# Second-layer heads of a hybrid decoder step: products of the new prompt state ahead of the value products, last sample state ahead of the norm work

## The reference, cut to what matters

```python
S = jnp.einsum('bhtd,bhsd->bhts', qc, kc) * jnp.exp(Dm - m_t[..., None])
num = jnp.einsum('bhts,bhse->bhte', S, vc) + ...      # value products
qn = jnp.sum(S, axis=-1) + ...                        # row sums
h = num / jnp.maximum(jnp.abs(qn), jnp.exp(-m_t))[..., None]
C_new = ... + jnp.einsum('bhsd,bhse->bhde', kc * decay[..., None], vc)   # new prompt state
n_new = ... + jnp.einsum('bhs,bhsd->bhd', decay, kc)                     # its row
```

## Time and profile before

| what | value |
|---|---|
| median of 3 runs | 1146.53 us (1138.76 to 1151.35) |
| profiled execution | 1140.05 us, its span 1138.3 us |
| TensorE busy | 1037.9 us (91%) |
| VectorE, ScalarE, GpSimd busy | 625.8 us, 401.9 us, 309.9 us |
| granted TensorE clock, mean | 0.959 |
| second layer's heads in the span | about 548 to 1032 us |

### The profile page before, as it was taken

How to read it: one execution, slowest core, us unless ns; L and a number is a source line. 1 busy time by engine, 2 the same in 40 slices (tenths; PEclk the granted TensorE clock), 3 DMA queues, 4 the chain that set the end, 5 groups by cost and what they waited for, 6 DMA issues and landing times. The chain is left out here.

```text
span 1138.3 us, 16176 instructions
## 1 busy us (share of the span) xinstructions
PE 1037.9 (91%) x5942; PEld 742.9 (65%) x5942; DVE 625.8 (55%) x1058; ACT 401.9 (35%) x705; POOL 309.9 (27%) x208
## 2 busy tenths in 40 slices
PE   5899999998679789998797999999999999997998
PEld 3677777775325489897575385847686587635776
DVE  4546767767343579996234563454345443446332
ACT  4434434432210323334445235432544344414210
POOL 5445444341000243441522223231513132110000
PEclk9999999999889789999899899999999999897999
DMA  9243455575491144453468754867468664744221
GB/s 250 71 123 97 131 138 132 146 198 171 127 306 57 38 83 150 156 177 139 141 201 294 280 190 142 284 237 254 160 203 288 215 214 152 271 147 149 75 74 75
DMA packets 167437, 191.75 MB, mean 168 GB/s; under 512 B 23638, under 2 KB 111558, under 8 KB 165798
## 3 DMA queue, kind: packets, MB, share of 16 engines
q1 hardware_dynamic: 154654, 159.15, 44.3%
q0 software_dynamic: 6000, 24.35, 7.1%
q10 hardware_dynamic: 6712, 7.29, 1.9%
HBM read 135.66 MB, written 55.22 MB: 168 GB/s over the span
## 5 line engine op out<-in xcount | busy, mean ns | idle before, releaser
L2125 PE MATMUL col_ps<-h_hi,ring_hi 128*128 128x260 f32 x448 | 130.3, 291 | 0.0
L2125 PE MATMUL col_ps<-h_hi,ring_lo 128*128 128x260 f32 x448 | 127.9, 286 | 0.0
L2125 PE MATMUL col_ps<-low,ring_hi 128*128 128x260 f32 x448 | 127.8, 285 | 0.0
L1978 DVE SCALAR_TENSOR_TENSOR state<-state,s_all,outer 128x1024 f32<-128x1024 f32 x64 | 86.0, 1372 | 74.5 <-ACT outer L1812 54.0
L648 PE MATMUL out_ps<-w_hi_a,h_hi_a 128*128 128x512 f32 x256 | 106.4, 416 | 5.5 <-POOL w_lo_a L469 5.5
L469 POOL TENSOR_TENSOR w_lo_a<-w_in,w_hi_a 128x1024 fp32r<-128x1024 f32 x32 | 87.2, 2746 | 79.6 <-ACT w_hi_a L344 40.5
L648 PE MATMUL out_ps<-w_lo_a,h_hi_a 128*128 128x512 f32 x256 | 101.2, 395 | 0.0
L648 PE MATMUL out_ps<-w_hi_a,h_lo 128*128 128x512 f32 x256 | 101.0, 395 | 0.0
L2125 PEld LDWEIGHTS col_ps<-h_hi,ring_hi 128*128 128x128 f32 x448 | 86.1, 192 | 12.9 <-issue 12.9
L1812 ACT ACTIVATE outer<-v_bcast,k_cols 128x512 f32<-128x512 f32 x128 | 81.8, 711 | 20.9 <-DMA v_bcast<-keep_v_rows 16.2
L1431 PE MATMUL xm_ps<-h_hi_c,w_col_hi 128*128 128x260 f32 x304 | 87.7, 288 | 0.0
(11 more groups left out here) (327 smaller groups left out, 2078.0 us busy)
## 6 DMA issues: line engine op xcount, KB each, us to landing
state<-in_state_C SPq DMA_DIRECT2D x64, 512.0 KB, 6.6
out_C_sample<-state SPq DMA_DIRECT2D x64, 512.0 KB, 5.5
w_in<-in_a_w_in SPq DMA_DIRECT2D x64, 256.0 KB, 5.7
ring_raw<-in_m_w_in POOLq DMA_DIRECT2D x28, 512.0 KB, 7.7
shared<-in_m_w_in SPq DMA_DIRECT2D x20, 512.0 KB, 5.1
k_head<-in_cache_k SPq DMA_DIRECT2D x128, 64.0 KB, 1.9
v_bcast<-keep_v_rows SPq DMA_DIRECT2D x32, 256.0 KB, 8.4
keep_xm_keep<-xm SPq DMA_DIRECT2D x4, 1040.0 KB, 6.9
```

Of the source, the lines that this page charges most:

```text
L1978: nc.vector.scalar_tensor_tensor(out=state[:, i % 4], in0=state[:, i % 4], scalar=s_all[:, 0, h, b:b + 1], in1=outer[:, g], op0=ALU.mult, ...
L2125: last = nc.tensor.matmul(col_ps[:, u % 4, 0:HALF], a[n % RING][:, k, :], b[:, k, s * HALF:(s + 1) * HALF], start=(k == 0 and j == 0), sto ...
```

## The change

Three edits, in the second layer's heads alone:

- TensorE: `prompt_state` d = 0 to 3 moves ahead of `values`. Sample `b0 + 4` is then multiplied after d = 1, head 0's samples 5 and 6 after d = 3, and sample 7 after the value product t = 1. The row of the new state leaves `prompt_state` and becomes `state_row`, after the value products and ahead of `sample_sum`. It waits for the first `norm_h` only.
- The numbers: `CP` comes ahead of `NUM`, and `TOK_TURNS` likewise. Bank parities stay. GpSimd's wait for `NUM + NT` thereby covers the prompt state's products as well.
- VectorE: `new_state` of sample 7, and in head 0 of sample 6, move ahead of `norm_h` t = 0.

ScalarE's program, SyncE's program and the number of instructions stay as they are.

```diff
-    NUM = OGT + TT
-    CP = NUM + NT
-    SNUM = CP + FH
+    CP = OGT + TT
+    NUM = CP + FH
+    SNUM = NUM + NT
...
                  + ["act"] * TT
+                 + ["act"] * FH
                  + ["dve"] * NT
-                 + ["act"] * FH
...
                 if h == 0:
                     new_state(h, 5)
+                    new_state(h, 6)
+                new_state(h, 7)
                 norm_h(h, 0)
                 norm_h(h, 1)
-                if h == 0:
-                    new_state(h, 6)
                 scale_h(h, 0)
                 norm_h(h, 2)
                 scale_h(h, 1)
                 norm_h(h, 3)
                 scale_h(h, 2)
-                new_state(h, 7)
                 scale_h(h, 3)
...
                 last.then_inc(toks_done, 1)
-                if d == 0:
-                    pe.wait_ge(*tok_count(h, NUM + NT - 1))
-                    for s in range(NT):
-                        last = nc.tensor.matmul(q_ps[0:1, :], one[:], kd[:, s, :], start=(s == 0), stop=(s == NT - 1))
-                    last.then_inc(n_done, 1)
+
+            def state_row(h):
+
+                pe.wait_ge(*tok_count(h, NUM))
+                for s in range(NT):
+                    last = nc.tensor.matmul(q_ps[0:1, :], one[:], kd[:, s, :], start=(s == 0), stop=(s == NT - 1))
+                last.then_inc(n_done, 1)
...
                 for t in range(TT):
                     turned_gate(h, t)
-                for t in range(NT):
-                    values(h, t)
-                    if t == 1:
+                for d in range(FH):
+                    prompt_state(h, d)
+                    if d == 1:
                         sample_q(h, b0 + 4)
                 if h == 0:
                     sample_q(h, 5)
                     sample_q(h, 6)
-                for d in range(FH):
-                    prompt_state(h, d)
-                    if d == 1:
+                for t in range(NT):
+                    values(h, t)
+                    if t == 1:
                         sample_q(h, 7)
+                state_row(h)
                 sample_sum(h)
```

## The result

The changed kernel takes 1158.5 us (median of 4 runs, 1157.2 to 1169.4), the kernel before 1142.6 (4 runs, three of them those shown ahead of the prediction). The ratio is 1.0158, 95% interval 1.011 to 1.0205: slower by about 1.6%, some 18 us. The prediction was 1151 us with a range of 1139 to 1161; the time lies in the range, but in the part above 1%, which had a chance of 0.13.

A forecast was written before the change was run, and what follows sets the result against it. TensorE's program was taken to set the pace (452.1 of 484.0 us busy over the heads). Head 0 +3.5, heads 1 to 3 +2.7, clock −1.7 gave +4.5 us: 1151.0 us on the median, range 1139 to 1161.

The forecast's parts named there:

- The wait removed: Head 0: TensorE's idle time ahead of the third value product goes, −3.7 us, and with it some clock.
- The banks in head 0: Prompt-state products d = 2 and d = 3 wait for ScalarE to empty their banks: 6.4 and 0.8 us.
- The clock behind the wait: Head 0: lowered clock on the d = 2 prompt-state product after the bank wait, 1.5 us (bounds 0 and 3.6).
- Sample 7 ahead of the norms: Head 0: sample 7's late state updates delay the norms on VectorE and so TensorE, 1.0 us (0 to 7.6).
- the slower rival: Head 0: sample 7's state load takes over 5 us, up to 10.6, holding the norms; 1158.6 us, chance 0.12.
- The sample norm copy: All heads: `sample_sum` waits for the copy behind the last norm and scaling; 1.5 us in head 0, 0.9 in others.
- My sign of being wrong: Listed signs: no idle ahead of L2248, an output-stage wait for `w_y`, or heads 1 to 3 growing over 2 us.
- The chain of 4.4 us: Time from last value product to `sample_sum` through last norm, root, scaling and copy; `state_row` covers 3.59 of it.
- The clock given back: Heads 1 and 3: row sums now stand between dense products, so half the clock loss returns, −1.7 us (0 to −3.4).
- where I took 0.7: Head 0: charge of 0.7 us for a second fall of the clock behind the row sums.
- That transposes bring the clock down whatever follows: Rival, all heads: the clock falls on prompt-state d = 0 after the gate's turns; +7.9 us, 1154.4 us, chance 0.14.
- Transfers moved later: Later loads of `xm` and, in the last head, `w_y` are covered, the latter by some 3 us; charged 0.

The follow-up runs named there:

- the run with the copies first: Changed kernel with ScalarE's copies out of the prompt-state banks ahead of the outer products of samples 6 and 7 in head 0; 1155.7 us, 1.0101 to the kernel before.
- split first: Changed kernel with GpSimd's split of a weight tile moved ahead of the four roots; 1152.2 us, ratio 1.0051 to the kernel before.
- the early copy: Changed kernel with VectorE's copy for the sample sum moved from behind the norms to behind the second norm; 1147.2 us, ratio 1.0011 to the kernel before.
- the run with the old head 0: Changed kernel with head 0 put back in the order of before, heads 1 to 3 in the new one; 1153.6 us, ratio 1.0064 to the kernel before.

## Why the prediction was right in kind and wrong in size

**The wait removed** went as written: 3.69 us fell to 0.38.

**The banks in head 0** were the right mechanism at nearly the right price: 6.62 us measured for 6.4, 0.52 for 0.8, with the broadcasts as the cause. That ScalarE's order behind them decides was shown by the run with the copies first. The clock behind the wait was under-charged: the third product took 6.08 us, 2.5 over its 3.6, where I took 1.5.

**Sample 7 ahead of the norms** was charged 1.0 us and took about 1.9: its two products and the waits of 0.41 and 0.38 us fill 650.87 to 653.72, which is 2.85 us, and the pair takes 0.98 in heads 1 to 3, where nothing is waited for. The last loads were issued at 643.45 and 644.47 us, and VectorE had them only at 647.99 and 650.98:

```profile
647.99 1.28 DVE L1978 SCALAR_TENSOR_TENSOR state<-state,s_all,outer 128x1024 f32<-128x1024 f32 x1 [12.98 <-DMA state<-in_state_C]
650.98 1.28 DVE L1978 SCALAR_TENSOR_TENSOR state<-state,s_all,outer 128x1024 f32<-128x1024 f32 x1 [1.70 <-DMA state<-in_state_C]
```

The second took 6.5 us, past the point of 5 us that I named for the slower rival. That rival's time, 1158.6 us, is what was measured, but not for its reason: it gave this load 6.6 us of delay, and it cost 0.9 more than the 1.0 charged. The upper end of the range was drawn past that rival, so that the time lies inside it is luck.

**The sample norm copy** is the step that failed. I charged 1.5 us in head 0 and 0.9 in each of the others, 4.2 in all; measured are 3.30, 2.92, 2.92 and 1.11, 10.3 us. My sign of being wrong, a stretch in heads 1 to 3 that grows by over 2 us, came in head 2 (31.8 to 35.0). The chain of 4.4 us was put together from a head in which the last scaling came after GpSimd's split, so it held no contention; I read the root's row and not the one behind it in GpSimd's order. Head 1 before, the split and the small step of the last scaling:

```profile
762.52 2.34 POOL L1682 TENSOR_TENSOR ring_lo<-ring_raw,ring_hi 128x1024 fp32r<-128x1024 f32 x1
768.15 0.15 DVE L2011 TENSOR_TENSOR rd<-rd,rstd_ln 128x1 f32<-128x1 f32 x1
```

In the new order the split starts exactly when the last scaling wants to run. In head 3, which has no split, the charge of 0.9 was nearly right (1.11), and so was the chain: from the end of the last value product (1034.2 us) to the end of the copy (1038.6) it took 4.5 us. That the split makes the rest was shown twice: split first brings the waits to about 1 us, and the early copy takes them away with the standstill still there. The Trainium skill states the rule in "SBUF — State Buffer", section "Who interferes with whom": VectorE and GpSimd share a pair of ports, a VectorE instruction with two SBUF inputs contends with a GpSimd instruction that reads SBUF, and the order of issue decides which of the two blocks. By it the wait was to be foreseen, and the trace agrees for L2011, 2.23 us beside a split of 2.34. The trace of before held such waits too, in another place (see the last section). With the split first the waits of heads 0 to 2 are 1.23, 0.94 and 0.84 us, so the split adds 2.07, 1.98 and 2.08, some 6.1 us; and the clock behind the longer waits, 0.62 and 0.60 over 4 us in heads 0 and 2 where it is 1.00 with the split first, adds about 1.5 us in each (0.4 of 4 us).

**The clock given back** was −1.7 us. In the changed kernel the clock fell behind the row sums in heads 0 and 3 and not in 1 and 2 (the first value products take 4.52, 2.82, 2.82 and 4.52 us); before, in 0, 1 and 3 (4.12, 4.38, 2.82 and 4.52). So head 1 won what I had counted, and head 0 paid 1.7 us where I took 0.7. That transposes bring the clock down whatever follows did not show: all the first prompt-state products run at full speed in heads 0 to 2 (7.13 us a pair), and nearly so in head 3 (7.36).

**Transfers moved later** cost nothing: the first output weights were issued at 1036.90 us and took 8.3 us to land, the output stage began at 1051.42, and no wait for them appears.

In sum, head 0 was forecast at 45.6 us and took 50.5: 1.8 us more at the sample sum, 1.0 for the clock on the third product, 1.0 behind the row sums, 0.9 at sample 7, together 4.7 of the 4.9. Heads 1 to 3 were forecast at +1.0 us in all. In the traces 434.1 − 417.9 − 8.4 = 7.8 us lie outside head 0's stretch, 1.1 of them in the columns behind it and 6.7 in heads 1 to 3; the run with the old head 0 has 7.3 for these heads.

## What to carry to other kernels

When products change places on one engine, the engines that empty their banks keep their old order: write out for each bank what stands ahead of its copy, and move the copies with the products. A wait that becomes late next has to be priced in its new neighbourhood: read what every other engine does in that microsecond, GpSimd's next instruction too, not only the lengths in the old place. A result that one late consumer needs (here a 0.68 us copy) goes ahead of a chain that it does not depend on.

## What the runs showed of the hardware

A split of a 128x1024 tile on GpSimd (2.34 us) held VectorE instructions with two SBUF tensors until it was over: a product of two 128x1 columns, started 0.13 us after the split, went from 0.15 to 2.23 us. It held a product of 128x512 in the same way. The kernel before shows that in the mixing of the head, which the change did not touch. L2027 multiplies two SBUF tensors and takes 0.69 us alone; beside a split it took 2.80 in head 0. L1926 reads one tensor from SBUF and one from PSUM, where TensorE's products lie; beside a split it took 0.42 us, as it does elsewhere. VectorE, then GpSimd:

```profile
672.48 2.80 DVE L2027 SCALAR_TENSOR_TENSOR gated<-xc_head,gated 128x512 f32<-128x512 f32 x1
676.34 0.69 DVE L2027 SCALAR_TENSOR_TENSOR gated<-xc_head,gated 128x512 f32<-128x512 f32 x1
681.25 0.42 DVE L1926 SCALAR_TENSOR_TENSOR gated<-scr,col_ps 128x260 f32<-128x260 f32 x1 [2.48 <-ACT scr L1776]
```

```profile
672.33 2.40 POOL L1682 TENSOR_TENSOR ring_lo<-ring_raw,ring_hi 128x1024 fp32r<-128x1024 f32 x1 [0.60 <-ACT ring_hi L1771]
681.02 2.39 POOL L1682 TENSOR_TENSOR ring_lo<-ring_raw,ring_hi 128x1024 fp32r<-128x1024 f32 x1 [2.70 <-ACT ring_hi L1771]
```

With the product in scalar form, which read one SBUF tensor and one column scalar and took 0.21 us beside the split, the next instruction was held instead, a scaling of a 128x512 tile with one SBUF tensor and two column scalars: 2.20 us for 0.55. I had not expected that of an instruction with one SBUF tensor. The Trainium skill, "SBUF — State Buffer", section "Who interferes with whom", names `tensor_scalar`, which this scaling is, among the operations that can take the shared pair when their operands meet conditions. No run here tests whether that is what holds it. One column scalar alone is not, since the product in scalar form ran on; the copy out of PSUM and the norm's statistics were not tested beside a split.
